# Down projection of an expert layer: all its weights split in two, its rows added by the scatter, its inputs gathered a block sooner

## The reference, cut to what matters

```
x   = x + concat(oA, oB) @ W_out
x   = x + HierMoE(RMSNorm(x))          # x before this line is called x1 below
y   = RMSNorm(x)

def expert_block(args):
    e, x_blk = args
    hidden = jax.nn.silu(x_blk @ exp_w_gate[e]) * (x_blk @ exp_w_up[e])
    return hidden @ exp_w_down[e]

y = yb.reshape(n_slots, D) * slot_gate[:, None]
out = jnp.zeros((T + 1, D), y.dtype).at[slot_tok].add(y)[:T]
```

## Time and profile before

| what | value |
|---|---|
| median of 3 runs | 1406.07 us (1398.72 to 1406.44) |
| the profiled execution | 1400.99 us, its span 1399.4 us |
| PE, DVE, ACT, POOL busy, whole span | 1234.6, 826.0, 684.7, 299.8 us |
| HBM read, written | 249.33 MB, 21.59 MB |
| PE busy, 780 to 1300 us | 509.94 of 520 us |
| wait in the page before the first gate matmul (L1809, for L1734) | 17.6 us |

### The profile page before, as it was taken

How to read it: one execution, slowest core, us unless ns; L and a number is a source line. 1 busy time by engine, 2 the same in 40 slices (tenths; PEclk the granted TensorE clock), 3 DMA queues, 4 the chain that set the end, 5 groups by cost and what they waited for, 6 DMA issues and landing times. The chain is left out here.

```text
span 1399.4 us, 17548 instructions
## 1 busy us (share of the span) xinstructions
PE 1234.6 (88%) x6388; PEld 922.8 (66%) x6388; DVE 826.0 (59%) x807; ACT 684.7 (49%) x757; POOL 299.8 (21%) x268
## 2 busy tenths in 40 slices
PE   3999999999899988599838999999999999999950
PEld 2867676767688768488726676676666766766730
DVE  5054545545366258253667667776677676677618
ACT  7154545454342243321226666666666656666513
POOL 0000000000211001000142244443344443344400
PEclk9999999999999995899959999999999999999985
DMA  5210101000211020331139999999999999999828
GB/s 166 60 31 16 31 16 30 16 16 1 59 33 31 1 91 31 128 150 62 45 118 386 353 356 358 355 355 352 350 350 363 346 365 347 351 359 360 292 65 327
DMA packets 67135, 263.22 MB, mean 188 GB/s; under 512 B 13344, under 2 KB 39056, under 8 KB 50704
## 3 DMA queue, kind: packets, MB, share of 16 engines
q1 hardware_dynamic: 54000, 214.23, 41.7%
q10 hardware_dynamic: 4320, 31.46, 5.5%
q0 software_dynamic: 8768, 16.87, 3.5%
HBM read 249.33 MB, written 21.59 MB: 194 GB/s over the span
## 5 line engine op out<-in xcount | busy, mean ns | idle before, releaser
L1809 PE MATMUL ps<-w_high,x_hi 128*128 128x512 f32 x512 | 211.7, 413 | 17.7 <-DVE x_lo L1734 17.6
L1809 PE MATMUL ps<-w_high,x_lo 128*128 128x512 f32 x512 | 203.4, 397 | 0.0
L1809 PE MATMUL ps<-w_lower,x_hi 128*128 128x512 f32 x512 | 203.1, 397 | 0.0
L1725 DVE TENSOR_TENSOR w_lower<-w_raw,w_high 128x2048 fp32r<-128x2048 f32 x62 | 141.7, 2285 | 50.0 <-ACT w_high L1653 50.0
L1752 DVE TENSOR_TENSOR s_lo<-w_s,s_hi 128x2048 fp32r<-128x2048 f32 x32 | 73.4, 2292 | 131.8 <-ACT s_hi L1674 131.8
L1730 DVE TENSOR_TENSOR w_lower<-w_raw,w_high 128x2048 fp32r<-128x2048 f32 x64 | 143.4, 2280 | 0.2 <-ACT w_high L1659 0.2
L420 DVE TENSOR_TENSOR_SCAN prod<-stay 128x256 f32<-128x256 f32 (+7 forms) x64 | 83.4, 1345 | 91.0 <-ACT beta L371 91.0
L1809 PEld LDWEIGHTS ps<-w_high,x_hi 128*128 128x128 f32 x512 | 98.0, 192 | 51.5 <-issue 29.2
L1653 ACT ACTIVATE w_high<-w_raw 128x2048 fp32r<-128x2048 f32 x62 | 118.6, 1912 | 11.6 <-DMA w_raw<-exp_w_gate 11.6
L1659 ACT ACTIVATE w_high<-w_raw 128x2048 fp32r<-128x2048 f32 x62 | 118.3, 1911 | 8.8 <-PE ps L1809 7.0
L1833 PE MATMUL ps<-w_d,hidT 128*96 128x512 f32 x256 | 116.8, 600 | 0.8 <-ACT hidT L1668 0.8
(11 more groups left out here) (258 smaller groups left out, 2365.0 us busy)
## 6 DMA issues: line engine op xcount, KB each, us to landing
w_raw<-exp_w_gate SPq DMA_DIRECT2D x32, 2048.0 KB, 9.2
w_raw<-exp_w_up SPq DMA_DIRECT2D x32, 2048.0 KB, 9.2
w_s<-exp_w_down SPq DMA_DIRECT2D x32, 1024.0 KB, 8.3
w_d<-exp_w_down ACTq DMA_DIRECT2D x30, 1024.0 KB, 10.4
w_raw<-w_in SPq DMA_DIRECT2D x25, 512.0 KB, 3.8
xt<-x SPq DMA_DIRECT2D x8, 512.0 KB, 6.6
w_raw<-w_out SPq DMA_DIRECT2D x8, 512.0 KB, 5.0
x_g<-x SPq DMA_DIRECT2D x8, 512.0 KB, 3.3
```

Source lines behind the costliest of these rows:

```text
L1725: dve.tensor_tensor(g_lo[:, part], w_g[:, part], g_hi[:, part].bitcast(F32), ALU.subtract).then_inc(glo, 1)
L1809: mm = pe.matmul(out, x_[:, n // 3, :], w_[:, n // 3, :], start=(n == 0), stop=(n == 3 * KD - 1))
```

## The change

The down weights are now split wholly: one tile `d_hi`, `d_lo` of four k-tiles, made in two halves (`d_split` on ACT and on DVE), and 24 float32r matmuls per block; the copy `hidT` is gone and `hT_hi` and `hT_lo` have all four k-tiles. The raw down weights lie in two whole buffers in the space of `cat`. To free that space `mix_and_route` writes x1 to `y_dram`, one row per token. SP alone loads down weights, 2 MB at once, two blocks ahead. The scatter adds its rows to `y_dram` (`compute_op=ALU.add`), and each scatter waits for the one before. The gather of block b+3 is issued in iteration b, where that of block b+2 was; that of block 2 is issued ahead of the loop. `turn_x` of block b+2 stands right behind `turn_h`, and `x_split` right behind `hid_copy` on ACT and `h_split` on DVE. `finish` takes the place of `combine`: one load per tile, the square and the root, and one scaling.

```diff
             for t in range(NT):
+                sp.wait_ge(x1_done, t + 1)
                 if t + 2 < NT:
-                    sp.wait_ge(x1_done, t + 1)
                     sp.dma_start(x[:, t % 2], a["x"][0, (t + 2) * P:(t + 3) * P, :]).then_inc(x_in[t % 2], 16)
+                sp.dma_start(pieces(k["y_dram"][t * P:(t + 1) * P, :]), x1(t)).then_inc(x1_out, 16)
                 sp.wait_ge(h2_done, t + 1)
                 sp.dma_start(k["h2_dram"][t * P:(t + 1) * P, :], h2[:, t % 2]).then_inc(h2_out[t % 2], 16)
...
+            sp.wait_ge(x1_out, 16 * NT)
...
-    wd, d_in, s_in = k["a"]["exp_w_down"][0], [sem(f"e_d_in{m}") for m in range(2)], sem("e_s_in")
+    wd, d_in = k["a"]["exp_w_down"][0], [sem(f"e_d_in{m}") for m in range(2)]
     HF = KF // 2
-    w_s = sb("w_s", [P, HF, D], F32, c)
-    s_hi, s_lo = (sb(n, [P, HF, D], F32R, c) for n in ("s_hi", "s_lo"))
-    w_d = sb("w_d", [P, 2, HF, D], F32, c)
-    hT_hi, hT_lo = (sb(n, [P, HF, CAP], F32R, c) for n in ("hT_hi", "hT_lo"))
+    w_d = [cat[:, KF * j:KF * (j + 1), :] for j in range(2)]
+    d_hi, d_lo = (sb(n, [P, KF, D], F32R, c) for n in ("d_hi", "d_lo"))
+    hT_hi, hT_lo = (sb(n, [P, KF, CAP], F32R, c) for n in ("hT_hi", "hT_lo"))
...
+            def down(j, e):
+                sp.dma_start(w_d[j], wd[bass.ds(e, 1)].rearrange("o (p k) n -> p (o k) n", p=P)).then_inc(d_in[j], 16)
...
-            sp.dma_start(w_s[:], wd[0].rearrange("(p k) n -> p k n", p=P)[:, 0:HF]).then_inc(s_in, 16)
-            down(0)
+            down(0, 0)
...
             sp.wait_ge(ulo, 2)
...
-            down(1)
...
             with sp.Fori(0, n_less) as i:
                 for j in range(2):
                     b = 2 * i + j
-                    e1 = sp.value_load(block_e[0:1, bass.ds(b + 1, 1)], min_val=0, max_val=EXPERTS - 1)
                     e2 = sp.value_load(block_e[0:1, bass.ds(b + 2, 1)], min_val=0, max_val=EXPERTS - 1)
                     sp.wait_ge(glo, 2 * b + 4)
                     load(sp, w_g, wg, e2, g_in)
-                    sp.wait_ge(slo, b + 1)
-                    sp.dma_start(w_s[:], wd[bass.ds(e1, 1)].rearrange("o (p k) n -> p (o k) n", p=P)[:, 0:HF])\
-                      .then_inc(s_in, 16)
+                    sp.wait_ge(dlo, 2 * b + 2)
+                    down(j, e2)
                     sp.wait_ge(ulo, 2 * b + 4)
                     load(sp, w_u, wu, e2, u_in)
...
-                pool.indirect_dma_start(k["y2_dram"][:, :], bass.IndirectOffsetOnAxis(ap=where[j][0:CAP, 0:1], axis=0),
-                                        y[j][0:CAP, :], None, bounds_check=2 * T - 1,
-                                        oob_is_err=False).then_inc(scattered[j], 16)
+                pool.indirect_dma_start(k["y_dram"][:, :], bass.IndirectOffsetOnAxis(ap=where[j][0:CAP, 0:1], axis=0),
+                                        y[j][0:CAP, :], None, bounds_check=T - 1, oob_is_err=False,
+                                        compute_op=ALU.add).then_inc(scattered[j], 16)
...
+            pool.wait_ge(gathered[0], 16)
+            name_rows(pool, lists, who, who_made, 0, slice(2, 3))
+            pool.wait_ge(who_made, 3)
+            pool.wait_ge(turned, 1)
+            gather(0)
...
-                    pool.wait_ge(gathered[j], 16 * i + 16)
+                    pool.wait_ge(gathered[1 - j], 16 * i + 16 + 16 * j)
...
-                    name_rows(pool, lists, who, who_made, j, bass.ds(b + 2, 1))
-                    pool.wait_ge(who_made, b + 3)
-                    pool.wait_ge(turned, b + 1)
+                    name_rows(pool, lists, who, who_made, 1 - j, bass.ds(b + 3, 1))
+                    pool.wait_ge(who_made, b + 4)
+                    pool.wait_ge(turned, b + 2)
                     pool.sem_inc(passed, 1)
-                    gather(j)
+                    gather(1 - j)
...
+                    pool.wait_ge(scattered[1 - j], 16 * i + 16 + 16 * j)
                     pool.wait_ge(y_done, b + 3)
                     pool.sem_inc(passed, 1)
                     scatter(j)
...
-                act.activation(hT_hi[:], turned_h()[:, 0:HF], ACT.Copy).then_inc(hidT_done, 1)
-                act.activation(hidT[:], turned_h()[:, HF:KF], ACT.Copy).then_inc(hidT_done, 1)
-
-            def s_split(b, first=False):
-                act.wait_ge(s_in, 16 * b + 16)
+                act.activation(hT_hi[:], turned_h(), ACT.Copy).then_inc(hidT_done, 1)
+
+            def d_split(b, j, loaded, m, first=False):
+                act.wait_ge(d_in[j], loaded)
                 if not first:
-                    act.wait_ge(d_used, b)
-                act.activation(s_hi[:], w_s[:], ACT.Copy).then_inc(shi, 1)
+                    act.wait_ge(d_used, 2 * b + m - 1)
+                part = slice(HF * m, HF * (m + 1))
+                act.activation(d_hi[:, part], w_d[j][:, part], ACT.Copy).then_inc(dhi, 1)
...
-                act.wait_ge(d_used, b + 1)
+                act.wait_ge(d_used, 2 * b + 2)
...
-            s_split(0, True)
+            d_split(0, 0, 16, 0, True)
+            d_split(0, 0, 16, 1, True)
             u_split(1, 0)
...
@@ -1698,22 +1700,21 @@
                     b = 2 * i + j
                     u_split(b + 1, 1)
                     hid_copy(b)
+                    x_split(b + 2, j)
                     g_split(b + 2, 0)
                     sigmoid(b + 1)
                     g_split(b + 2, 1)
+                    d_split(b + 1, 1 - j, 16 * i + 16 + 16 * j, 0)
                     evict(b, j, i)
-                    e2 = act.value_load(block_e[0:1, bass.ds(b + 2, 1)], min_val=0, max_val=EXPERTS - 1)
-                    act.dma_start(w_d[:, j], wd[bass.ds(e2, 1)].rearrange("o (p k) n -> p (o k) n", p=P)
-                                  [:, HF:KF]).then_inc(d_in[j], 16)
-                    s_split(b + 1)
-                    x_split(b + 2, j)
+                    d_split(b + 1, 1 - j, 16 * i + 16 + 16 * j, 1)
                     u_split(b + 2, 0)
...
-                dve.wait_ge(hidT_done, 2 * b + 2)
-                dve.tensor_tensor(hT_lo[:], turned_h()[:, 0:HF], hT_hi[:].bitcast(F32), ALU.subtract).then_inc(hTlo_done, 1)
-
-            def s_split(b):
-                dve.wait_ge(shi, b + 1)
-                dve.tensor_tensor(s_lo[:], w_s[:], s_hi[:].bitcast(F32), ALU.subtract).then_inc(slo, 1)
+                dve.wait_ge(hidT_done, b + 1)
+                dve.tensor_tensor(hT_lo[:], turned_h(), hT_hi[:].bitcast(F32), ALU.subtract).then_inc(hTlo_done, 1)
+
+            def d_split(b, j, m):
+                dve.wait_ge(dhi, 2 * b + m + 1)
+                part = slice(HF * m, HF * (m + 1))
+                dve.tensor_tensor(d_lo[:, part], w_d[j][:, part], d_hi[:, part].bitcast(F32), ALU.subtract).then_inc(dlo, 1)
...
                     u_split(b + 1, 1)
                     h_split(b)
+                    x_split(b + 2, j)
                     g_split(b + 2, 0)
                     gate_mul(b + 1)
                     g_split(b + 2, 1)
-                    s_split(b + 1)
-                    x_split(b + 2, j)
+                    for m in range(2):
+                        d_split(b + 1, 1 - j, m)
...
-            def down(b, j, loaded):
-                pe.wait_ge(hidT_done, 2 * b + 2)
+            def down(b):
+                pe.wait_ge(hidT_done, b + 1)
+                pe.wait_ge(hTlo_done, b + 1)
                 pe.wait_ge(y_done, b + 2)
-                pe.wait_ge(d_in[j], loaded)
-                for f in range(HF):
-                    for m in range(D // HALF):
-                        cols = slice(m * HALF, (m + 1) * HALF)
-                        pe.matmul(ps[0:CAP, 2 + m, :], hidT[:, f, :], w_d[:, j, f, cols], start=(f == 0), stop=False)
-                pe.wait_ge(hTlo_done, b + 1)
-                pe.wait_ge(slo, b + 1)
-                for f in range(HF):
-                    for n, (x_, w_) in enumerate(((hT_hi, s_hi), (hT_hi, s_lo), (hT_lo, s_hi))):
+                for f in range(KF):
+                    if f % HF == 0:
+                        pe.wait_ge(dlo, 2 * b + f // HF + 1)
+                    for n, (x_, w_) in enumerate(((hT_hi, d_hi), (hT_hi, d_lo), (hT_lo, d_hi))):
                         for m in range(D // HALF):
                             cols = slice(m * HALF, (m + 1) * HALF)
-                            mm = pe.matmul(ps[0:CAP, 2 + m, :], x_[:, f, :], w_[:, f, cols], start=False,
-                                           stop=(f == HF - 1 and n == 2))
-                mm.then_inc(d_used, 1)
+                            mm = pe.matmul(ps[0:CAP, 2 + m, :], x_[:, f, :], w_[:, f, cols], start=(f == 0 and n == 0),
+                                           stop=(f == KF - 1 and n == 2))
+                    if f % HF == HF - 1:
+                        mm.then_inc(d_used, 1)
...
@@ -1855,10 +1857,10 @@
                     pe.wait_ge(gated, b + 1)
                     gate_rows(b + 1, 1 - j, 0, 15)
                     turn_h(b)
+                    turn_x(j, 16 * i + 32)
```

(22 more changed lines are left out.)

80 lines of the change are left out of this document (28 added, 52 removed).

## The result

The changed kernel takes 1393.88 us (median of 6 runs, 1390.31 to 1400.93) against 1406.38 us before (1398.72 to 1408.42, 6 runs): ratio 0.9922, 95% interval 0.9892 to 0.9951. It is 0.8% faster, where 3.1% was forecast, and 1362 us with the range 1349 to 1386 is missed by 8 us at its upper end. The profiled execution took 1391.23 us, its span is 1389.6 us.

What follows compares the result with a forecast made beforehand. PE was taken to bound the loop, DVE the last stage. Span 1399.4 + 6 - 31.3 - 0.6 - 0.1 + 1.5 - 17 = 1357.9, plus 1.6 around it and half of 5 us: 1362 us, range 1349 to 1386.

Steps and rivals of the forecast that it cites:

- The transfers: Expert loop: DMA work of 16.2 to 19.3 us a block against a period of 18.12, lower half taken.
- rival A: Loop: DMA becomes the bound, with 18.9 us a block +23 us, 1385 (1374 to 1396); chance 0.20.
- What bounds the kernel now: Before the change PE bounds the expert loop, 19.20 us a block; DVE bounds the last stage.
- Down on split weights: Loop, down projection: 24 split matmuls take 5.58 us instead of 6.20, -0.62 us per block on PE.
- The rows turned sooner: Loop: PE's wait of 0.57 us for the low part of the rows goes, 0.11 comes back.
- Do the handwritten orders still fit?: Loop: nothing that PE waits for is late; least slack 0.8 us, for the hidden rows' low part.
- The first gather: Start of the loop: PE stands until 757 to 759 us for block 2's gather; +6 us (+3 to +12).
- Mixing stage and the tail: Mixing stage: x1 stores 0, at most +2 us. End: last scatter +1.5, last stage -17 (13 to 19).
- The rule of the page: Loop: HBM limit of about 358 GB/s for one core against the loop's 355, so nothing there could gain.
- rival B: Loop: mean rate capped at 355 GB/s, 19.9 us a block, +52 us, 1414; chance 0.05.
- The sum: Whole kernel: span 1357.9 us from all terms, 1359.5 with 1.6 around it, 1362 with half of 5 us added.
- Rival C: Loop: the wait moves as DVE or POOL runs late; PE stands 0.57 us again, +17, 1379; chance 0.15.

Runs made afterwards that it cites:

- e16: e15 with a plain scatter that overwrites instead of adding (sums are lost): 1356.2 us.
- e15: e13 without one of the down projection's three passes, so less work on PE and part of the result missing; adding scatter kept: 1383.2 us.
- e10: e8 with a scatter that adds, x1 also written into both rows of each token: 1390.4 us.
- e17: e5 with each down load issued as two loads of 1 MB on SyncE's queue, gate and up loads whole: 1388.2 us.
- e8: The kernel before with only the rows gathered and turned sooner and the first gather early; half of down plain, scatter plain: 1383.0 us.
- e2: The changed kernel loading only half of a block's down weights in the loop (1 MB of 2; results wrong): 1361.7 us.
- e18: e14 with each down load in two pieces too; computes the whole reference: 1367.1 us.
- e4: The changed kernel with block 2's gather issued before the four small DMAs that GpSimd waits for: 1387.3 us.
- e5: e4 with GpSimd naming a block's places and weights ahead of the gather, not behind it: 1391.7 us.
- e1: The changed kernel with a plain scatter that overwrites instead of adding (sums are lost), every wait kept: 1360.7 us.
- e7: e5 with two rows per token written by a plain scatter, x1 in its own memory, sums made at the end; computes the layer: 1375.7 us.
- e13: e5 with the gate and up loads each cut into two loads of 1 MB, a half issued once its space is free: 1385.6 us.
- e14: e7 with the gate and up loads each cut into two halves: 1371.5 us.
- e3: The changed kernel with the loop's down loads issued by ACT on its own queue, early in the iteration, instead of by SP: 1396.5 us.
- e9: e7 with the first sum of the last stage on GpSimd instead of VectorE: 1384.6 us.

## Why the prediction was wrong

**The step that failed is *The transfers*.** It put a block's work for the DMA engines at 16.2 to 19.3 us against a period of 18.12 and took the lower half. With the engines full it was 18.26 us with a plain scatter (e16) and 19.15 with the adding one (e15), 18.87 in the changed kernel; over all runs with the adding scatter with whole down loads, the engines were busy for 18.1 to 19.1 us a block, at no time less than the forecast's period of 18.12. The argument from rates misled: 438 GB/s in 2 us and 413 over 20 us are rates of other mixes of transfers, and no run of the loop held more than 380. The simpler reading that I had as rival A, share times period, 0.94 x 19.20 = 18.0, was right within 0.3. Of the same step, "0 to 1.3 us, 0.6 taken" for adding measured 0.73 to 0.89. And "starts are hidden behind the load in front" did not help: the engines were busy for 0.99 of the loop, not idle between loads, and each load landed later (up 12.4 us, 9.2 before).

**Rival A came, with its number.** It gave 18.9 us per block, with a chance of 0.20; 18.87 was measured. That it fits so closely is partly luck, as the periods of other runs with the same bytes and the adding scatter go from 18.53 (e10) to 19.17 (e17). Against the forecast that is 29 x 0.75 = 21.8 us. Its total of 1385 is exceeded by the two terms below.

**What bounds the kernel now** was right for before (e8, with a wait of PE gone and 0.67 us less per block, gained at once and ran PE at 520 of 520 us), but too short for after. "PE is the bound" says nothing of how near the next one is, and the change took 1.3 us from the one while it put 0.7 to 0.9 on the other.

**Down on split weights and *The rows turned sooner*.** Right in mechanism and slightly mis-sized in our favour: PE's block is 17.87 (e2, e18), not 18.12; 19.20 - 17.87 = 1.33 where 1.08 was forecast. e8 measures the part of the rows alone as 0.67 (forecast 0.46). The rest, 0.66, is the down weights' (forecast 0.62).

**Do the handwritten orders still fit?** Yes, once the loads are there: e2 and e18 have no stall of PE in 520 us.

**The first gather.** +6 was forecast, with +3 to +12. Block 1's transposes came 15.3 us later, 5.9 of it from the mixer's clock: +9.4. The gather landed in 12.6 us (11.2 taken), so PE's transposes are at 765.65, 1.0 us later than 758.7 + 5.9; from there to block 1's transposes it took 19.3 us, 17.3 forecast, part of it at the lower clock. In e4 and e5 block 2 stands 5.1 and 4.2 us sooner for the early gather; by the medians no gain of e5 on the changed kernel is shown.

**Mixing stage and the tail.** The extra stores of x1 cost nothing visible. The last scatter's landing cost +1.7 (forecast +1.5), the last stage -16.3 (forecast -17); DMA was at 416 GB/s and 1.02 there, as said.

**The rule of the page.** The Trainium skill, "DMA: Bandwidth & Descriptors", section Specifications, has about 358 GB/s of HBM for one core. The changed kernel held 360, e15 357, but e1, e16 and e18 held 373, 374 and 380 over 520 us: with the plain scatter the rule's ceiling is passed by 6%, and the time of rival B, built on it, did not come. With the uncounted reads of the adding scatter the changed kernel is at about 374 GB/s too (an estimate, above), so that a limit on the mean rate, which is rival B's mechanism, is seen, but at 371 to 380 GB/s, where it costs far less than B's 52 us.

**The sum.** 1359.5 + 21.8 (period) + 3.4 (gather) + 5.9 (the mixer's clock) + 0.2 and 0.7 (tail) = 1391.5, against 1391.23 of the profiled execution. The mixer's clock is no part of the change, and the forecast's last step, half of 5 us added for it, was right in kind.

**Rival C** had 0.15. It was not what held the changed kernel, where e1 recovers the pace with POOL's order untouched, but one moved gather (e4) was enough to bring it about.

## What to carry to other kernels

When a change speeds the bounding engine, take the second resource's share times the period as its block, not its bytes over the best rate seen elsewhere; 0.94 left 1.2 us, and the change wanted 1.3 and put 0.9 on it. Treat the result as a range: here the engines' busy time for the same bytes moved by 0.4 us with the plain scatter and by 1.0 with the adding one. Cost what a cheaper last stage does to the loop: adding in the DMA saved 16 us once and cost 25 us in the loop and some more around it, and two rows per token written plainly were 18 us better (e7). On a queue served in order, the place of a load is set by the wait ahead of it; move loads so that the queue never runs empty. Handing a single buffer back in pieces is worth a try: it went with 1367.1 us in e18, though its gain alone, in e13 and e14, is not clear of the spread. And when a transfer reads as well as writes, ask whether the profile's GB/s has both.

## What the runs showed of the hardware

- A 4 KB packet of the adding scatter took 327 ns in the trace's records, twice the 159 of a plain one; the last scatter's issue on GpSimd took 1.44 us against 0.92 before, and it landed in 5.3 us against 3.6. The rows that it adds to stand in no count of what was read (245.52 MB read with and without adding).
- The same weights cost the engines different times: 16.5 us per block in e16, 16.7 in e15, 16.05 in e10, which fitted with an adding scatter into 18.53 us. Packet size does not explain it (e17); what does is open. e10 differs also in that its down loads are spread over two queues and two moments of the block, and e3 shows that a second queue alone is not it.
- GpSimd's cast of the places, 0.2 us at its shortest in the kernel before, took 7.7 us on the mean in e4, where it runs beside DVE's subtractions, and DVE's scaling went from 1.28 to 2.00 us on the mean beside GpSimd's adds (e9). The Trainium skill, "GPSIMD Engine Reference", section Specifications, names the shared port; that it can lock a loop into a stable slower cycle, in which no wait for a DMA stands, is this case's.
- PE's granted clock in a stage of unchanged code was 0.50 in one execution and 0.69 in another, and moved all that follows by 6 us.
